# Opening in halves without a wait for parameters, four modulation tiles moved behind the sums of later norms, first column groups chunk by chunk

## What is computed

```python
def trunk_layer(x, c, mixing, w_ada, b_ada, norm_w, ffn_up, ffn_down):
    mod = (jax.nn.silu(c) @ w_ada + b_ada).reshape(c.shape[0], N_MOD, 1, D_MODEL)
    sh1, sc1, g1, sh2, sc2, g2, sh3, sc3, g3 = [mod[:, i] for i in range(N_MOD)]
    h = x + 0.5 * g1 * swiglu(rmsnorm(x, norm_w[0]) * (1 + sc1) + sh1, ffn_up[0], ffn_down[0])
    mix_out, *state = mixing(rmsnorm(h, norm_w[1]) * (1 + sc2) + sh2)
    h = h + g2 * mix_out
    h = h + 0.5 * g3 * swiglu(rmsnorm(h, norm_w[2]) * (1 + sc3) + sh3, ffn_up[1], ffn_down[1])
    return h, state
```

## Time and profile before

| | us |
|---|---|
| median of 3 runs (lowest, highest) | 961.89 (959.0, 969.99) |
| span of the profiled execution | 961.2 |
| PE busy, share of the span | 885.5 (92%) |
| weight loads | 746.0 (78%) |
| DVE | 503.5 (52%) |
| ACT | 316.2 (33%) |
| POOL | 101.1 (11%) |

### The profile page before, as it was taken

How to read it: one execution, slowest core, us unless ns; L and a number is a source line. 1 busy time by engine, 2 the same in 40 slices (tenths; PEclk the granted TensorE clock), 3 DMA queues, 4 the chain that set the end, 5 groups by cost and what they waited for, 6 DMA issues and landing times.

```text
span 961.2 us, 18054 instructions
## 1 busy us (share of the span) xinstructions
PE 885.5 (92%) x6658; PEld 746.0 (78%) x6658; DVE 503.5 (52%) x978; ACT 316.2 (33%) x503; POOL 101.1 (11%) x182
## 2 busy tenths in 40 slices
PE   4689999999998999989999968899897999999996
PEld 2378898988898898876656534666777999999995
DVE  1335545445353747546666565657446555554433
ACT  1423333333323434544333611000225333333311
POOL 2000000000011000122222232330110000000011
PEclk9879999999999899999999988999998999999998
DMA  9949897877655241357768699997390555443301
GB/s 306 371 145 381 281 311 247 310 252 273 243 206 204 85 151 49 131 187 254 261 213 274 212 325 328 325 322 281 99 341 9 175 176 176 163 147 130 130 1 50
DMA packets 122464, 204.78 MB, mean 213 GB/s; under 512 B 7564, under 2 KB 56998, under 8 KB 122274
## 3 DMA queue, kind: packets, MB, share of 16 engines
q1 hardware_dynamic: 105280, 163.08, 49.6%
q0 software_dynamic: 11648, 38.45, 11.7%
q10 hardware_dynamic: 5474, 2.39, 1.0%
HBM read 199.01 MB, written 4.88 MB: 212 GB/s over the span
## 4 chain that ended last, share of the span: by engine, by line
PE 84%; DVE 6%; DMA 4%; ACT 2%; issue 2%; ACTq 1%; POOLq 0%; SPq 0%; POOL 0%; DVEq 0%
PE bank L714 18%; PE bank L715 18%; PE bank L716 18%; PE bank L678 8%; PE bank L925 3%; PE bank L1161 3%; PE bank L696 3%; PE bank L965 2%; DMA wring<-in_w_ada 2%; PE bank L744 2%; DMA kv<-in_cache_v 1%; DVE wring_rounded L1482 1%; ACTq L1410 1%; PE bank L1110 1%; DMA region<-in_state_conv 1%
## 5 line engine op out<-in xcount | busy, mean ns | idle before, releaser
L714 PE MATMUL bank<-hn_rounded,kv_rounded 128*128 128x288 f32 x928 | 281.8, 304 | 21.0 <-DVE xs_rounded L1526 10.6
L715 PE MATMUL bank<-xs_rounded,kv_rounded 128*128 128x288 f32 x928 | 277.3, 299 | 0.0
L716 PE MATMUL bank<-hn_rounded,wring_rounded 128*128 128x288 f32 x928 | 276.3, 298 | 0.0
L1482 DVE TENSOR_TENSOR wring_rounded<-wring,kv_rounded 128x1024 fp32r<-128x1024 f32 (+1 forms) x164 | 187.6, 1194 | 73.0 <-ACT kv_rounded L1222 72.9
L1222 ACT CAST kv_rounded<-wring 128x1024 fp32r<-128x1024 f32 (+1 forms) x164 | 158.7, 1027 | 162.9 <-PE bank L716 114.6
L714 PEld LDWEIGHTS bank<-hn_rounded,kv_rounded 128*128 128x128 f32 x928 | 176.8, 190 | 33.1 <-issue 13.8
L716 PEld LDWEIGHTS bank<-hn_rounded,wring_rounded 128*128 128x128 f32 x928 | 178.1, 192 | 0.0
L715 PEld LDWEIGHTS bank<-xs_rounded,kv_rounded 128*128 128x128 f32 x928 | 177.9, 192 | 0.0
L714 PE MATMUL bank<-region_rounded,kv_rounded 128*128 128x288 f32 x352 | 104.6, 297 | 0.8 <-DVE modT L1471 0.8
L715 PE MATMUL bank<-region_rounded,kv_rounded 128*128 128x288 f32 x352 | 103.8, 295 | 0.0
L716 PE MATMUL bank<-region_rounded,wring_rounded 128*128 128x288 f32 x352 | 103.5, 294 | 0.0
(11 more groups left out here) (256 smaller groups left out, 979.9 us busy)
## 6 DMA issues: line engine op xcount, KB each, us to landing
wring<-in_ffn_up SPq DMA_DIRECT2D x44, 1024.0 KB, 7.7
wring<-in_w_ada SPq DMA_DIRECT2D x36, 1024.0 KB, 10.7
wring<-in_ffn_down SPq DMA_DIRECT2D x16, 1024.0 KB, 7.3
kv<-in_cache_v SPq DMA_DIRECT2D x64, 256.0 KB, 4.7
kv<-in_cache_v POOLq DMA_DIRECT2D x64, 256.0 KB, 4.9
wring<-in_w_in SPq DMA_DIRECT2D x14, 1024.0 KB, 6.8
kv<-in_cache_k SPq DMA_DIRECT2D x44, 256.0 KB, 4.4
kv<-in_cache_k POOLq DMA_DIRECT2D x44, 256.0 KB, 4.6
```

Source lines behind the costliest of these rows:

```text
L714: nc.tensor.matmul(out, hi, rhs_hi, start=start, stop=False)
L715: nc.tensor.matmul(out, hi, rhs_lo, start=False, stop=False)
L716: return nc.tensor.matmul(out, lo, rhs_hi, start=False, stop=stop)
L1482: v.tensor_tensor(wringR[:, slot, c, :], wring[:, slot, c, :], whiR[:, u % 2, c, :], ALU.subtract).then_inc(s_wlo, 1)
```

## The change

It has four parts. (1) SP no longer waits for the parameters. PE transposes x first, then multiplies ada 0, transposes the parameters, sums the squares, and only then multiplies ada 1. The list `ADA_COL` lets ada tile 1 fetch the columns of sc1's first half and tile 2 those of sh1's second half, so that tiles 0 and 1 serve chunks 0 to 3 and tiles 2 and 3 chunks 4 to 7; the norm's coefficients, scaled chunks and remainders are made for four chunks at a time, with ada 2 and 3 multiplied in between. (2) The loop of up and ada tiles handles ada 4 to 13, its first round being written out. (3) Ada 14 and 15 move out of the loop, and 16 and 17 out of the first down product: 14 and 15 are multiplied behind the sums of norm 1, 16 and 17 behind those of norm 2, and in the list `tiles` they stand ahead of w_in 0 and of up 0 of the second feed-forward. (4) The first up tile behind norms 0 and 2, and the first four columns of w_in behind norm 1, run chunk by chunk over all four columns (`up_first`, and the loop over `turn`), in four banks. ACT's four small loads (`wab`, `ptab`, `pab`) move behind the second gate; the ring slot that the attention borrows (`extra`) and the buffers laid over the ring move by one slot with the list.

The core of the diff:

```diff
+ADA_LOOPED = 14
...
-        tiles = [("ada", j) for j in range(ADA_FIRST)] + [("up", 0, 0), ("ada", 4), ("ada", 5)]
+        ADA_COL = [0, 2, 1, 3] + list(range(ADA_FIRST, ADA_TILES))
+        tiles = [("ada", 0), ("ada", 1), ("up", 0, 0), ("ada", 2), ("ada", 3)]
...
-        tiles += [("down", 0, 0, 0), ("ada", 16), ("down", 0, 0, 1), ("ada", 17), ("down", 0, 0, 2)]
-        tiles += [("down", 0, 1, t) for t in range(3)]
+        tiles += [("down", 0, g, t) for g in range(2) for t in range(3)]
+        tiles += [("ada", 14), ("ada", 15)]
         tiles += [("in", j) for j in range(7)]
+        tiles += [("ada", 16), ("ada", 17)]
         tiles += [("up", 1, j) for j in range(UP_TILES)]
...
-            load(0)
-            sp.wait_ge(s_par, 16 * 6)
-            for n in range(1, LOOP + 4):
+            for n in range(LOOP + 4):
                 load(n)
...
+            def up_first(l, ks):
+
+                slot, side = number[("up", l, 0)] % RING, (S1ST * l) % 2
+                for k in ks:
+                    normed(2 * l, k)
+                    if k % 2 == 0:
+                        pe.wait_ge(s_wlo, 4 * S1ST * l + k // 2 + 1)
+                    for s in range(2 if k < KD - 2 else 1):
+                        for half in range(2):
+                            up_products(s, half, k, slot, side)
+                if ks[-1] == KD - 1:
+                    for k in (KD - 2, KD - 1):
+                        for half in range(2):
+                            up_products(1, half, k, slot, side)
...
             pe.wait_ge(s_cT, 1)
-            for j in range(ADA_FIRST):
-                ada_mm(j, *tile(("ada", j)))
-                if j == 0:
-                    features()
-                if j:
-                    ada_T(j - 1, (j - 1) % 2)
+            ada_mm(0, *tile(("ada", 0)))
+            features()
+            pe.wait_ge(s_h, KD)
             sumsq(0)
+            pe.wait_ge(s_pv, 1)
+            ada_mm(1, *tile(("ada", 1)))
+            ada_T(0, 0)
+            ada_T(1, 1)
+            up_first(0, range(4))
+            ada_mm(2, *tile(("ada", 2)))
+            ada_T(2, 0)
+            ada_mm(3, *tile(("ada", 3)))
             ada_T(3, 1)
-            up_tile(0, 0, number[("up", 0, 0)] % RING, 0, first=True)
-            ada_mm(4, *tile(("ada", 4)))
-            ada_mm(5, *tile(("ada", 5)))
-            ada_T(4, 0)
+            up_first(0, range(4, KD))
...
             sumsq(1)
-            for turn in range(29):
+            ada_mm(14, *tile(("ada", 14)), bank=5)
+            ada_mm(15, *tile(("ada", 15)), bank=6)
+            for k in range(KD):
+                normed(1, k)
+                if k % 2 == 0:
+                    pe.wait_ge(s_wlo, 4 * IN0 + k // 2 + 1)
+                for turn in range(4):
+                    m = in_products(turn, turn, k)
+                    if k == KD - 1:
+                        m.then_inc(s_win, 1)
+            ada_T(14, 0, bank=7)
+            ada_T(15, 1, bank=5)
+            for turn in range(4, 29):
...
             sumsq(2)
-            for j in range(3):
-                up_tile(1, j, number[("up", 1, j)] % RING, (S1ST + j) % 2, first=(j == 0))
+            ada_mm(16, *tile(("ada", 16)), bank=5)
+            ada_mm(17, *tile(("ada", 17)), bank=6)
+            up_first(1, range(KD))
+            ada_T(16, 0, bank=7)
+            ada_T(17, 1, bank=5)
+            for j in range(1, 3):
+                up_tile(1, j, number[("up", 1, j)] % RING, (S1ST + j) % 2)
...
+            ada_copy(0, 0)
+            inverse_rms(0)
+            ada_copy(1, 1)
+            for c in range(4):
+                if c % 2 == 0:
+                    round_quarters(0, (c // 2,))
+                rounded_hn(0, c)
+            round_quarters(0, (2, 3))
+            ada_copy(2, 0)
+            ada_copy(3, 1)
+            for c in range(4, KD):
+                rounded_hn(0, c)
...
+            for half in range(2):
+                for j in (2 * half, 2 * half + 1):
+                    mod_tile(j, j % 2)
+                dve.wait_ge(s_mod, 2 * half + 2)
+                coefficients(0, slice(4 * half, 4 * half + 4))
+                dve.wait_ge(s_rstd, 1)
+                normalised(0, slice(4 * half, 4 * half + 4), weights=None if half else 0)
...
             residual(0, (UP_TILES + 5, IN0))
```

More of the change, by code:

```diff
@@ L214, in build_program @@
         pa = carver(wflat)
+        pa(4096)
         ktok = pa(3, 512)
@@ L818, in _ @@
-            ada_T(15, 1)
-            pe.wait_ge(s_modr, 15)
+            pe.wait_ge(s_x, 32)
+            for c in range(KD):
+                if c >= 4:
+                    pe.wait_ge(s_h, c - 3)
+                for t in range(3):
+                    n = P if t < 2 else NS
+                    m = T(ps[c % 4][:, t * P:t * P + n], xin[0:n, t, c * P:(c + 1) * P], n)
+                m.then_inc(s_xT, 1)
+            pe.wait_ge(s_cT, 1)
+            ada_mm(0, *tile(("ada", 0)))
+            features()
@@ L1242, in ada_copy @@
                     act.wait_ge(s_adaT, j - 1)
-                nc.scalar.copy(adasb[:, odd, :], ps[4 + odd][:, :]).then_inc(s_adaev, 1)
+                nc.scalar.copy(adasb[:, odd, :], ps[4 + odd if bank is None else bank][:, :]).then_inc(s_adaev, 1)
             def gate_silu(l, f, odd):
@@ L1421, in _ @@
             norm(2)
+            ada_copy(16, 0, bank=5)
+            ada_copy(17, 1, bank=6)
             for j in range(3):
@@ L1482, in rest_quarters, with smp4, coefficients @@
                     v.tensor_tensor(wringR[:, slot, c, :], wring[:, slot, c, :], whiR[:, u % 2, c, :], ALU.subtract).then_inc(s_wlo, 1)
+            tail_cols = slice(SEQ, TOK)
+            def smp4(x, ks):
+                return x[:, ks, tail_cols].rearrange("p c (b t) -> p c b t", b=NB)
+            def coefficients(ni, ks):
+                n = ks.stop - ks.start
+                own(v.scalar_tensor_tensor(coef[:, ks, :], modT[:, (3 * ni + 1) * KD + ks.start:(3 * ni + 1) * KD + ks.stop, :], 1.0,
+                                           nw[:, KD * ni + ks.start:KD * ni + ks.stop].unsqueeze(2).to_broadcast([P, n, NR]), ALU.add, ALU.mult))
+                own(v.tensor_tensor(smp4(hn, ks), smp4(h, ks), coef[:, ks, 1:NR].unsqueeze(3).to_broadcast([P, n, NB, NT]), ALU.mult))
@@ new lines, in normalised, with scaled, rest @@
+            def normalised(ni, ks, weights=None):
+                n = ks.stop - ks.start
+                sh = modT[:, 3 * ni * KD:(3 * ni + 1) * KD, :]
+                def scaled(c):
+                    v.scalar_tensor_tensor(xs[:, c, 0:SEQ], h[:, c, 0:SEQ], coef[:, c, 0:1], rstd[:, 0:SEQ], ALU.mult, ALU.mult).then_inc(s_xs, 1)
+                def rest(c):
+                    dve.wait_ge(s_hn, KD * ni + c + 1)
+                    v.scalar_tensor_tensor(xsR[:, c, 0:SEQ], xs[:, c, 0:SEQ], sh[:, c, 0:1], hnR[:, c, 0:SEQ], ALU.add, ALU.subtract).then_inc(s_xl, 1)
+                first = ks.start
+                scaled(first)
+                own(v.tensor_tensor(xs[:, ks, tail_cols], hn[:, ks, tail_cols], rstd[:, tail_cols].unsqueeze(1).to_broadcast([P, n, NS]), ALU.mult))
+                scaled(first + 1)
+                own(v.tensor_tensor(smp4(xs, ks), smp4(xs, ks), sh[:, ks, 1:NR].unsqueeze(3).to_broadcast([P, n, NB, NT]), ALU.add))
+                scaled(first + 2)
+                own(v.tensor_copy(hnR[:, ks, tail_cols], xs[:, ks, tail_cols]))
+                rest(first)
+                v.tensor_tensor(xsR[:, ks, tail_cols], xs[:, ks, tail_cols], hnR[:, ks, tail_cols], ALU.subtract).then_inc(s_hs, 1)
+                if weights is not None:
+                    rest_quarters(weights, (0,))
+                for c in range(first + 1, ks.stop):
+                    if c + 2 < ks.stop:
+                        scaled(c + 2)
+                    rest(c)
+                    if weights is not None:
+                        rest_quarters(weights, (c,))
@@ L1908, in _ @@
                 hidden(1, 2 * j + 1, 1)
+                if j == 0:
+                    mod_tile(16, 0, bank=7)
+                    mod_tile(17, 1, bank=5)
             with dve.Fori(0, 2) as i:
```

226 lines of the change are left out of this document (91 added, 135 removed).

## The result

| | kernel before | changed kernel |
|---|---|---|
| median of 20 runs each on the same chip, us | 961.04 | 965.24 |
| lowest, highest | 957.72, 969.99 | 961.74, 974.02 |
| span of the profiled execution | 961.2 | 963.6 |
| ratio to the kernel before, 95% interval | | 1.0039, 1.002 to 1.0057 |

The account below looks back on a forecast made before the run. PE was taken as the bound, busy for most of 961.2 us; terms 0.0 - 5.5 + 5.6 + 2.0 = +2.1 gave a span of 963.3, plus 0.7 a time of 964, range 951 to 971.

Parts of the forecast that it names:

- Sums of norm 0: Opening: the sums of squares end at 31.6 us (29.8 to 33.8) instead of 40.03, 8.4 earlier.
- From the sums to the release of up 0: Opening: from the end of norm 0's sums at 31.6 to the end of the first up tile at 68.5.
- high clock throughout: Rival, faster: the clock stays high in the opening, first up tile ends at 57, 952 us in all; chance 0.08.
- E: End of the opening's first up tile, forecast at 68.5 us, bounds 57 (high clock) and 79 (low clock).
- Up 2 and up 3: Opening: these two tiles load late, so their first columns end 4.4 and 2.4 us late; opening 0.0 in all.
- Out of down: -5.5: First down product: two modulation tiles leave it, saving 5.5 us (5.1 to 5.9).
- Norm 1: +5.6: Norm 1: w_in 0 is loaded later, DVE's residual waits behind its remainders, sums 5.9 late; 5.6 us lost.
- T: Release of the second-last down tile before norm 1, when w_in 0 is loaded; 296.0 in the kernel before.
- Norm 2: +2.0: Norm 2: up 0 lands later, sums 3.8 late, part regained behind them; 2.0 us lost (0.9 to 2.9).
- At nothing: Parts counted as 0: chunk-by-chunk order (at most 2 us lost, gain excluded), SP's dropped parameter wait, ACT's moved small issues.
- Late tiles hidden: Rival, faster: DVE and ACT have the late tiles in time, 947.5 us in all; chance 0.10.
- Clock low throughout: Rival, slower: the low clock holds through both halves of the opening, E = 79, 974.5 us in all; chance 0.12.

Follow-up runs that it names:

- the state loads moved: Changed kernel with ACT's four loads of the recurrent state issued behind the eighth block instead of the fourth; 958.88 us, ratio 0.9963.
- fillers: Products nobody reads, put into the opening's two pauses of the changed kernel; with 10 and 7 of them and the loop's loads in another order: 958.57 us.
- the loads reordered: Changed kernel with both up tiles loaded ahead of both modulation tiles each round, the constants behind the loop; 964.04 us, ratio 1.0008.
- tiles earlier: Changed kernel with w_in 0 loaded ahead of ada 15, and the second feed-forward's up 0 ahead of ada 16 and 17; 957.2 us, ratio 0.9952.
- residual first: Changed kernel with DVE's remainders of w_in 0 and the second feed-forward's up 0 placed behind all eight residual chunks; 955.28 us, ratio 0.9929.
- first join: Changed kernel with w_in 0 and up 0 loaded earlier, the loop's loads in the other order, and 19 and 15 filler products; 960.62 us, ratio 0.9992.
- long fillers: Changed kernel with 19 and 15 products that nobody reads put into the opening's two pauses; 963.13 us, ratio 1.0016.

## Why the prediction was right, and where it was not

**Sums of norm 0.** Forecast 31.6 (29.8 to 33.8), measured 28.84. The sums began 1.0 earlier (the parameters' transposes took 1.35 where I put 2) and took 4.15, all at the high rate, where I put 5.9. This step failed by 2.8, and it is all that the opening gained over the forecast. But the larger part is a draw of the clock: in a run whose code is the same up to here (the one with the state loads moved) the 16 products took 7.01, and up 0 was released at 69.4. Its row of the timeline (the granted clock is recorded only from 31.6 on in that trace, so the level is told by the products' length):

```profile
25.80 7.01 PE L764 MATMUL bank<-xs,const 128*128 128x288 f32 x16
```

Over the eleven traces the root behind the sums started between 28.6 and 32.9. The bounds should have been those of the row at each clock, 4.05 and 8.1, counted from 24.7: 28.8 to 32.8.

**From the sums to the release of up 0.** Forecast 8.7 to the first product, then 8.7, 6.7, 3.9 and 8.9, 36.9 in all; measured 8.7, 9.2, 6.5, 4.0 and 8.1, 36.6. Every term held. The rival with the high clock throughout did not occur without fillers; neither did the low one. For its bounds of E, 57 and 79, the prediction shows no working: with fillers both halves ran at the high clock and E was 62.05.

**Up 2 and up 3.** Forecast late by 4.4 and 2.4; PE stood 3.1 and 1.8. The landings themselves were as forecast (up 2 at 79.45, that is E + 14.0 with E = 65.4), and up 3 was released at E + 50.1 against a forecast of E + 49.7. The four pauses are not all of it: with the loads reordered, the stretch from E to the release of up 3 took 44.7, of which 1.45 is the wait for ada 4, so 43.3 without late tiles. The late tiles cost 6.8 in all, the sum of the forecast's 4.4 and 2.4; 4.9 stand in the pauses, the rest in gaps between products too short for the view to list as waits. Reordered loads took the pauses away, so their cause is shown.

**Out of down: -5.5.** Measured -5.6.

**Norm 1: +5.6.** The sums were forecast at T + 19.3 and came at T + 19.2, by the mechanism named: two runs removed it, one by the landing and one by DVE's order. But two errors cancel in the 19.2. The tile landed at 295.6, T + 8.0 where I had T + 9.2, and the second half of the sums took 3.90 in place of 2.1, since PE had stood for 3.8 and the granted clock from 302.9 to 306.3 was 0.51, which I had not counted.

Behind the sums I wrote about 20 to the fifth column, 0.3 less than before. The terms beside it add up to more: the gap of 5.3, 12.8, 1 to 2 for the clock and 1.3 make 20.4 to 21.4. It came at 20.8, 0.7 later than before, so the terms held and their sum was wrong. The clock took 1.5 of it, since with the tiles earlier the fifth column begins at 19.3. The stretch in the changed kernel, PEclk 0.80 where the run with the tiles earlier has 1.00:

```profile
302.50:320.00 17.50, 14.99 (x85) 10.85 (x86) 12.29 (x32) 9.76 (x16) 2.31 (x4) 0.80 0.70 254
```

That the pause inside the sums is what brings the clock down behind them is not shown: the run with the residual first has no such pause, and its fifth column still begins at 21.0, with PEclk 0.93 from 297.5 to 322.0.

**Norm 2: +2.0.** Right in size, by errors that cancel. The terms written there, 3.8 and 19.7 in place of 21.1, add up to 2.4 and not 2.0. The sums were late by 1.9 where I had 3.8, since up 0 landed at 716.7 though all had moved by 1.2 (two modulation tiles ahead of it took less time than two of `ffn_up`, the case that I had given as 2.7). Behind the sums nothing was gained: up 0 was released 0.8 sooner after them, and the transposes of ada 16 and 17 that follow gave it back.

**At nothing.** The wait for parameters and the chunk-by-chunk order: both held within what can be measured.

**The mixer: not in the sum.** The change moves no instruction there (the buffers that lie over the ring moved by one slot), and I put no term for it. It moved by 3.0. In the ten traces with this code (before, changed, and eight of the experiments) the stage takes 307.4 to 313.1, so 3.0 is within what it varies. The traces show where they part: the first 168 us agree within 0.3 us in all ten. The rest of the stage, before and then changed, in the columns of the earlier trace rows:

```profile
548.84:688.82 139.98, 117.25 (x964) 77.62 (x963) 87.93 (x206) 14.98 (x40) 35.27 (x64) 0.91 0.81 282
546.99:690.02 143.03, 116.65 (x964) 75.78 (x963) 87.94 (x206) 14.93 (x40) 35.17 (x64) 0.92 0.79 276
```

Between these two PE's standing differs, 22.7 against 26.4, and not its work. Over the ten traces this rest takes 139.4 to 145.1, with PEclk 0.93 in the three shortest and 0.88 to 0.92 in the others. The wait for the exponential does not part them by itself: it is 10.9 to 11.5 in those three as well. The four with a stage of 307.4 to 308.0 (before, tiles earlier, residual first, first join) are those whose sums of norm 1 end at T + 13.5; but as all ten agree for 168 us behind that, a link is not shown, and what makes PE's pauses and clock differ there stays open. A forecast that rests on one trace should have carried this stage's scatter in its range.

**From span to time.** I added 0.7, the distance of three runs' median from the span of one traced execution. That execution lay above its kernel's median; the changed kernel's runs are 2.0 longer than their spans, so 963.3 stands for 965.3. The measured 965.24 agrees with the sum of the terms by the luck told above.

**The rivals.** Late tiles hidden: no, they cost what was said, and where an edit hides them the time falls. Clock low throughout: no. The forecast's case came out: gains and losses cancel.

## What to carry to other kernels

Before a load is moved back in a ring, list what each engine has queued behind the instruction that consumes it: here the cost was not PE waiting for weights but four unrelated residual chunks behind a remainder on DVE, and changing that order alone was worth 1.1%. A pause of PE costs itself and can cost the products behind it at half rate: here that followed pauses of 5.2 and 4.0, and not those of 1.8 and 1.3 in up 2. Filling it with work that nobody reads pays only if the filler's length is read from a row. Reordering a queue moves a late transfer to the next place, so follow each moved load to the next tile that it stands ahead of.

## What the runs showed of the hardware

**The instant at which the clock rises is a draw.** With the same instructions ahead, the sums took 4.15 in eight of the eleven traces, all at the high rate, and 5.5 to 7.1 in three (the reordered loads, the long fillers, the state loads), where the rate rose on the way, near 31.7 in the last. The release of up 0 came at 64.9 to 69.5 where no fillers stood ahead of it. The Trainium skill, TensorE: Matmul & The Clock Gate, Part 1, says too that the count of slow products differs from run to run of one kernel; the traces agree, with 4.15 against 7.01 for the same 16.

**Issuing loads held an engine for 13 us.** ACT's four loads of the state kept it from 566.5 to 579.4 (575.7 + 3.75), one issue taking 7.93, while pages of the cache were on their way. The view by line, in the changed kernel: duration in ns, least, median and most, and the first and last start:

```profile
L1459 ACTq DMA_DIRECT2D region<-in_state_gdn x3: 404/785/7926, 566.5 to 567.7; - x3
L1459 ACTq DMA_DIRECT2D const<-in_state_gdn x1: 3750/3750/3750, 575.7 to 575.7; - x1
```

An engine with urgent arithmetic behind it is the wrong one to issue from at such a time.
